# Two units of the joined stage and two of the last feed-forward stage multiplied ahead of their norm

## The chip, the cores and the metric

The kernel runs on one core of one Trainium2 chip. The metric is device time in microseconds of one execution; the time of a kernel is the median of its runs.

## The reference

The reference is three blocks of a transformer on 512 tokens of width 1024, in float32: a block with stick-breaking attention, a block with dilated attention, and a block with adaptive modulation whose mixer joins a gated recurrence (HGRN2) and differential attention. What matters here is the third block (`rmsnorm` divides by the root of the mean square and multiplies a gain):

```python
x = _rmsnorm(h, norm_final)                     # end of the first two blocks
mod = jax.nn.silu(c) @ w_ada[l] + b_ada[l]
sh1, sc1, g1, sh2, sc2, g2 = jnp.split(mod[:, None, :], N_MOD, axis=-1)
u = rmsnorm(h, norm1_w[l]) * (1.0 + sc1) + sh1
proj = u @ w_in[l]                              # f, q, i, g, v, d, k of four heads
...
h = h + g1 * mix
u = rmsnorm(h, norm2_w[l]) * (1.0 + sc2) + sh2
ff = (jax.nn.silu(u @ w_ffn_gate[l]) * (u @ w_ffn_up[l])) @ w_ffn_down[l]
h = h + g2 * ff
```

Every product of the form (norm(h) * scale + shift) @ W has the same value as rstd * ((h * scale) @ W) + shift @ W, since rstd is one number per token.

## The kernel before

Activations lie feature-major: `h`, `xh` and `xl` are eight tiles of 128 features by 512 tokens. A "unit" is a 128-column slice of a weight matrix (1024 x 128, eight blocks of 128 x 128). Each operand is split in a rounded high part and a residue: ScalarE writes `whi` (L334, `split_hi`), VectorE or GpSimd writes `wlo` (L345, `split_lo`), and `product` (L348) issues three matmuls for each block: high by high (L360), high weights by low data (L361), low weights by high data (L362). So a unit is 24 matmuls of 512 columns. Units pass through a ring of three or four slots of `raw`, `whi` and `wlo`; SyncE loads `raw` (L278, L291) when the residue of the unit two before is done. The order on each engine is the order in which its program is written out; semaphores join the engines. `ahead` splits a unit two units before its product.

The phases in order are qkv, o_a, gu0, down0, qkvb, o_b, gu1, down1, duo, mix, gu2, down2. In `down1` (24 units of the second block's feed-forward, three for each tile of `h`) ScalarE and VectorE also form the modulation vector `mod` (`ada_scale`, `ada_product`, `ada_tile`), ScalarE squares each new tile twice (L896, L897) and GpSimd adds the squares up. PE then sums them over the partitions (L758, L760), and from both sums VectorE and ScalarE form `twin`, the root of the two norms in a row (`twin_dve`, `twin_root_act`). `modulate_dve` (L929) multiplies `h` by scale and twin tile by tile, `modulate_act` (L943) adds the shift and writes `xh`, and `lower_dve` (L937) writes `xl`. PE's first unit of duo, f, waits for each tile.

`duo` is the joined stage: four heads with units f, q, i, g, v, d, k. VectorE forms the gates of the recurrence (`gate_first` L1657, `gate_rest`, `scan`), the differences for the decays (`difference`, L1688), and ScalarE the decays (L1297, L1298) and the copies of the products out of PSUM (`unit_out`, L1245). PE turns the copies of i and v (L2064). Behind head 0's sweep the matmuls of the levels (L2009) follow. GpSimd forms a query product (L1101).

`mix` has eight units, one for each tile of `h`; the first four have most of their matmuls done early. `res_dve` (L679) multiplies the old tile by the joined norm (L693), waits for the product and writes the new tile (L700); `res_act` (L658) squares it (L427); GpSimd adds (L457). PE sums (L480), and VectorE (L497, L504, L506, L509) and ScalarE (L485, L487) form `rstd`. The modulation of eight tiles follows as above, and the first unit of `gu2` waits for each tile (`ffn_pe`). `gu2` has eleven rounds of four units (gate, up, gate, up) of which `ffn_dve` and `ffn_act` form the activations.

Of the kernel before, what the change touches and what calls it, by code (L numbers as in the profile page):

```python
# [77 lines left out]
class Units:  # L78
# [3 lines left out]
    def __init__(self, weights, count, body, ring, before, used, widths=None):  # L82
        self.weights, self.count, self.body, self.ring = weights, count, body, ring
        self.first, self.used = before, list(used)
        self.widths = widths or [KT] * body
        self.last = False

# [10 lines left out]
    def slot(self, j):  # L98
        return j % self.body % self.ring
# [7 lines left out]
def build(nc, a, out):  # L107
    ctx = ExitStack()
    with ctx:
# [31 lines left out]
        small = place("small", [P, 96], F32)  # L141
        nc_wada = top[0]
# [7 lines left out]
        plain = [place(f"plain{m}", [P, S], F32, base + 16 * KIB + 2 * KIB * m)[:, :] for m in range(KT)]  # L150
        gained = [place(f"gained{m}", [P, S], F32, base + 32 * KIB + 2 * KIB * m)[:, :] for m in range(KT)]
# [12 lines left out]
        work = small[:, 66:96]  # L164

# [52 lines left out]
        twin = place("twin", [P, S], F32, where["yh"])  # L218
# [16 lines left out]
        oraw = put("oraw", [P, S], F32)  # L235
        amat = place("amat", [P, NB, P], F32, nc_wada)
# [15 lines left out]
        for name, count, body, ring in (("qkv", 8, 3, 3), ("o_a", 2, 4, 4), ("gu0", 11, 4, 4), ("down0", 4, 6, 3),  # L252
# [8 lines left out]
            u.order = (1, 2, 0) if name == "qkvb" else None  # L261
        phases[-1].last = True
# [85 lines left out]
        def product(pe, u, t, j, bank, hi, lo, k0=0, start=True, stop=True, ready=None, midway=None, part=None):  # L348
# [65 lines left out]
        r1a, r1f = Residual(), Residual(scaled=False, alone=False)  # L414
        r2a, r2f = Residual(scaled=False), Residual(scaled=False)

        def residual_hi(act, r, m, gain):
# [6 lines left out]
            act.activation(xh[:, m], h[:, m], ACT.Copy, scale=column(gain, m)).then_inc(r.x_hi.sem, 1)  # L424

# [33 lines left out]
        def twin_squares_pool(pool):  # L459
# [8 lines left out]
            for m in range(KT):  # L468
                load_ada(3 * m + 2, 3 * m + 5)
                if 1 <= m < KT - 1:  # L470
# [3 lines left out]
                    for sums in (plain, gained):  # L474
                        pool.tensor_tensor(sums[0], sums[0], sums[m], ALU.add).then_inc(twin_added, 1)
# [116 lines left out]
        y_hi, y_lo = sem("y_hi"), sem("y_lo")  # L592
        twin_squared, twin_added = sem("twin_squared"), sem("twin_added")
# [64 lines left out]
        def res_act(act, u, r, gain, rooted=True, begun=0, ada=None):  # L658
            per = 1 if u.body == 4 else 3

            def body(t, end=False):
                for j in range(u.body):
                    if not leading(t) or j >= begun:
                        split_hi(act, u, ahead(u, t, j, end))
                    if ada is not None:
                        ada_scale(act, ada, t, j)
                    if j % per == per - 1:
                        m = t * (u.body // per) + (j // per)
                        residual_hi(act, r, m, gain)
                        residual_sq(act, r, m, (j // per) % 2)  # L670
            body(0)
# [7 lines left out]
        def res_dve(dve, u, r, gain, modulation=None, ada=None, regain=None, refined=True, begun=0, banks=EARLY):  # L679
            per = 1 if u.body == 4 else 3  # L680

            def body(t, end=False):
                for j in range(u.body):
                    if not leading(t) or j >= begun:
                        split_lo(dve, u, ahead(u, t, j, end))
                    final = end and j == u.body - 1
# [16 lines left out]
                    if ada is not None and final:  # L703
                        ada_product(dve, ada, t, j)
            body(0)
# [14 lines left out]
        def res_pe(pe, u, r, hi, lo, ready, ada=None, sum_now=True, twin=False, early=0, banks=EARLY):  # L720
# [35 lines left out]
            if twin:  # L756
                pe.wait_ge(twin_squared, 2 * KT - 1)
                pe.matmul(ps[:, 7], ones[:, :], plain[KT - 1], start=False, stop=True).then_inc(twin_total.sem, 1)  # L758
                pe.wait_ge(twin_squared, 2 * KT)
                pe.matmul(ps[:, 6], ones[:, :], gained[KT - 1], start=False, stop=True).then_inc(twin_total.sem, 1)  # L760
# [3 lines left out]
        def ffn_act(act, u, f):  # L764
            def body(t):
                for j in range(4):
                    split_hi(act, u, ahead(u, t, j, False))
                    if j % 2:
# [3 lines left out]
                        act.activation(tmp[i][:, :], tmp[i][:, :], ACT.Silu).then_inc(f.silu.sem, 1)  # L772
                        hold(act, f.prod, n)
                        act.activation(acth[:, 2 * t + i], tmp[2 + i][:, :], ACT.Copy).then_inc(f.hi.sem, 1)  # L774
            with act.Fori(0, u.count) as t:
                body(t)

        def ffn_dve(dve, u, f, scaled=True):
            def body(t):
                for j in range(4):  # L780
                    split_lo(dve, u, ahead(u, t, j, False))
                    if j % 2:
# [4 lines left out]
                        if scaled:  # L787
# [8 lines left out]
                        dve.tensor_tensor(tmp[2 + i][:, :], tmp[i][:, :], tmp[2 + i][:, :], ALU.mult).then_inc(f.prod.sem, 1)  # L796
# [19 lines left out]


# [69 lines left out]
        def twin_squares_act(act, u, r):  # L887

            def body(t, end=False):
                for j in range(u.body):  # L890
                    split_hi(act, u, ahead(u, t, j, end))
                    ada_scale(act, 1, t, j)
                    if j % 3 == 2:
                        m = t * 2 + j // 3
                        wait(act, r.h_new, m + 1)
                        act.activation(plain[m], h[:, m], ACT.Square).then_inc(twin_squared, 1)  # L896
                        act.activation(gained[m], h[:, m], ACT.Square, scale=column("final1", m)).then_inc(twin_squared, 1)  # L897
# [10 lines left out]
        def twin_dve(dve, r):  # L908
# [5 lines left out]
            dve.scalar_tensor_tensor(twin[:, :], ps[:, 6], 1.0 / D, var[:, :], ALU.mult, ALU.add).then_inc(twin_var.sem, 1)  # L914
            wait(dve, twin_root, 2)
# [7 lines left out]
        def modulate_dve(dve, key, scale, shift, factor):  # L923

            for m in range(KT):
# [5 lines left out]
                if m:  # L931
                    lower_dve(dve, key, shift, m - 1)
            lower_dve(dve, key, shift, KT - 1)

        def lower_dve(dve, key, shift, m):
# [4 lines left out]
        def modulate_act(act, key, shift):  # L940
# [1343 lines left out]
```

## Time and profile before

| | us |
|---|---|
| median of 3 runs | 1973.14 (1970.89 to 1973.36) |
| profiled execution | 1972.97 |
| its span, first to last instruction | 1970.8 |
| PE busy | 1904.0 (97%) |
| VectorE busy | 1082.2 (55%) |
| ScalarE busy | 928.4 (47%) |
| GpSimd busy | 138.5 (7%) |

The mean granted clock of PE is 0.989 of 2.4 GHz. "PE busy" counts matmuls that overlap by their pipelined ends, so a share of 97% does not say that PE has only 3% to lose. Times in the rows are microseconds from the start of the span; a row of the timeline has start, duration, engine, line, operation, output and inputs, count, and in brackets the idle time of the engine before it with what ended that time. In the chain of waits a row has start, duration and what.

### The profile page before, as it was taken

To read this page: it belongs to the slowest core of one execution; us is meant where nothing else is said; L and a number is where in the kernel's file an instruction comes from. 1 tells how busy PE (TensorE), PEld (TensorE's weight loads), DVE (VectorE), ACT (ScalarE), POOL (GpSimd) and SP (SyncE) were. 2 spreads that over 40 slices of the span, in tenths; PEclk is the share of its full clock that TensorE was granted. 3 is DMA by queue.
4 is the path that set the end of the run, shared out by engine and by line. 5 is a ranking of instruction groups with operands and counts; after the bars stand their busy time and mean duration, and the time that the engine had idled before them with its cause. 6 is when DMAs were issued, how large, how long until landed. Compare 5 with 4: busy or idle time off the path is not lost.

```text
span 1970.8 us, 25056 instructions
## 1 busy us (share of the span) xinstructions
PE 1904.0 (97%) x8914; PEld 1533.2 (78%) x8914; DVE 1082.2 (55%) x1640; ACT 928.4 (47%) x1520; POOL 138.5 (7%) x132
## 2 busy tenths in 40 slices
PE   7999999999999899999999999889999879999997
PEld 6777778888788677778888878668887658888886
DVE  5566554444466767755444455577776554444322
ACT  5555543323477444444434367556555344343322
POOL 0000020000021000010000013211011100000000
PEclk9999999999999999999999999999999989999999
DMA  3111123232455322223232355511122122323331
GB/s 136 65 64 64 43 93 103 93 103 89 134 195 192 105 86 90 87 76 99 86 105 85 104 170 189 183 64 58 66 70 65 65 74 86 105 85 104 89 98 62
DMA packets 56478, 193.65 MB, mean 98 GB/s; under 512 B 7136, under 2 KB 7648, under 8 KB 56416
## 3 DMA queue, kind: packets, MB, share of 16 engines
q1 hardware_dynamic: 47712, 163.60, 25.5%
q0 software_dynamic: 7696, 27.79, 4.3%
q10 hardware_dynamic: 1008, 1.45, 0.2%
q8 instruction: 37, 0.61, 0.1%
q14 instruction: 25, 0.20, 0.0%
HBM read 186.52 MB, written 2.10 MB: 96 GB/s over the span
## 4 chain that ended last, share of the span: by engine, by line
PE 92%; DVE 3%; ACT 2%; issue 1%; DMA 1%; SPq 0%; ACTq 0%; POOL 0%; DVEq 0%
PE ps L360 27%; PE ps L361 26%; PE ps L362 26%; PE ps L2009 1%; PE ps L1896 1%; PE ps L956 1%; PE ps L1877 1%; PE ps L981 1%; PE ps L1912 1%; PE ps L971 1%; PE ps L1900 1%; DVE xl L937 1%; PE ps L2057 0%; PE ps L2044 0%; PE ps L2083 0%
## 5 line engine op out<-in xcount | busy, mean ns | idle before, releaser
L360 PE MATMUL ps<-xh,whi 128*128 128x512 f32 x1536 | 608.5, 396 | 22.9 <-DVE xl L937 16.6
L362 PE MATMUL ps<-xh,wlo 128*128 128x512 f32 x1536 | 600.7, 391 | 0.0
L361 PE MATMUL ps<-xl,whi 128*128 128x512 f32 x1536 | 600.3, 391 | 0.0
L345 DVE TENSOR_TENSOR wlo<-raw,whi 128x1024 fp32r<-128x1024 f32 (+1 forms) x296 | 365.5, 1244 | 231.3 <-ACT whi L334 225.7
L334 ACT ACTIVATE whi<-raw 128x1024 fp32r<-128x1024 f32 (+1 forms) x304 | 312.0, 1036 | 170.0 <-PE ps L362 169.1
L360 PEld LDWEIGHTS ps<-xh,whi 128*128 128x128 f32 x1536 | 289.8, 189 | 93.1 <-issue 16.8
L362 PEld LDWEIGHTS ps<-xh,wlo 128*128 128x128 f32 x1536 | 289.9, 189 | 61.3
L361 PEld LDWEIGHTS ps<-xl,whi 128*128 128x128 f32 x1536 | 290.1, 189 | 59.6 <-issue 1.4
L360 PE MATMUL ps<-acth,whi 128*128 128x512 f32 x528 | 213.0, 403 | 0.0
L362 PE MATMUL ps<-acth,wlo 128*128 128x512 f32 x528 | 208.6, 395 | 0.0
L361 PE MATMUL ps<-actl,whi 128*128 128x512 f32 x528 | 208.3, 394 | 0.0
L772 ACT ACTIVATE tmps<-tmps 128x512 f32<-128x512 f32 x66 | 41.7, 632 | 306.8 <-DVE tmps L788 207.3
L457 POOL TENSOR_TENSOR sqsum<-sqsum,tmps 128x512 f32<-128x512 f32 x39 | 52.0, 1333 | 951.2 <-ACT tmps L427 951.2
L362 PEld LDWEIGHTS ps<-acth,wlo 128*128 128x128 f32 x528 | 99.3, 188 | 23.3
L361 PEld LDWEIGHTS ps<-actl,whi 128*128 128x128 f32 x528 | 99.6, 189 | 21.4 <-issue 0.2
L360 PEld LDWEIGHTS ps<-acth,whi 128*128 128x128 f32 x528 | 99.6, 189 | 21.3 <-issue 0.2
L788 DVE TENSOR_TENSOR tmps<-ps,rstd 128x512 f32<-128x512 f32 x44 | 30.4, 692 | 133.3 <-PE ps L362 133.3
L360 PE MATMUL ps<-oh,whi 128*128 128x512 f32 x192 | 78.6, 409 | 6.5 <-DVE wlo L345 3.5
L798 DVE TENSOR_TENSOR actl<-tmps,acth 128x512 f32 (+1 forms) x66 | 45.7, 693 | 65.2 <-ACT acth L774 65.2
L361 PE MATMUL ps<-ol,whi 128*128 128x512 f32 x192 | 77.1, 402 | 0.0
L362 PE MATMUL ps<-oh,wlo 128*128 128x512 f32 x192 | 76.7, 400 | 0.0
L774 ACT ACTIVATE acth<-tmps 128x512 f32 x66 | 41.7, 632 | 66.3 <-DVE tmps L796 66.3
(296 smaller groups left out, 2230.8 us busy)
## 6 DMA issues: line engine op xcount, KB each, us to landing
raw<-in_gu SPq DMA_DIRECT2D x132, 512.0 KB, 3.3
raw<-in_down SPq DMA_DIRECT2D x48, 512.0 KB, 3.7
raw<-in_qkv SPq DMA_DIRECT2D x24, 512.0 KB, 4.3
wada<-in_ada POOLq DMA_DIRECT2D x24, 512.0 KB, 3.7
tmps<-in_ada POOLq DMA_DIRECT2D x24, 512.0 KB, 3.6
raw<-in_qkvb SPq DMA_DIRECT2D x24, 512.0 KB, 3.6
raw<-in_down SPq DMA_DIRECT2D x24, 384.0 KB, 3.1
raw<-in_recur SPq DMA_DIRECT2D x16, 512.0 KB, 3.3
```

Source lines behind the costliest of these rows:

```text
L334: act.activation(whi[:, s, 0:n], raw[:, s, 0:n], ACT.Copy).then_inc(hi_done, 1)
L345: eng.tensor_tensor(wlo[:, s, 0:n], raw[:, s, 0:n], whi[:, s, 0:n].bitcast(F32), ALU.subtract).then_inc(lo_done, 1)
L360: pe.matmul(ps[:, bank], whi[:, s, w], hi[:, k0 + k], start=start and k == 0, stop=False)
L361: pe.matmul(ps[:, bank], whi[:, s, w], lo[:, k0 + k], start=False, stop=False)
L362: mm = pe.matmul(ps[:, bank], wlo[:, s, w], hi[:, k0 + k], start=False, stop=stop and k == n - 1)
L457: pool.tensor_tensor(sqsum[:, :], sqsum[:, :], sq[m % 2][:, :], ALU.add).then_inc(r.added.sem, 1)
L772: act.activation(tmp[i][:, :], tmp[i][:, :], ACT.Silu).then_inc(f.silu.sem, 1)
L774: act.activation(acth[:, 2 * t + i], tmp[2 + i][:, :], ACT.Copy).then_inc(f.hi.sem, 1)
L788: dve.tensor_tensor(tmp[i][:, :], ps[:, 2 * i], rstd[:, :], ALU.mult).then_inc(f.gate.sem, 1)
L798: dve.tensor_tensor(actl[:, 2 * t + i], tmp[2 + i][:, :], acth[:, 2 * t + i].bitcast(F32), ALU.subtract).then_inc(f.lo.sem, 1)
L937: dve.scalar_tensor_tensor(xl[:, m], tmp[m % 2][:, :], mod[:, shift + m:shift + m + 1], xh[:, m].bitcast(F32), ALU.add, ALU.subtract).then ...
L956: pe.matmul(tri_ps[i][:, OFF[b]:OFF[b] + w], q[rows, c * P:(c + 1) * P], k[rows, 0:w], start=True, stop=True, skip_group_check=True)\
```

## The change

Two units of `duo` (f and q of head 0) and two units of `gu2` (the first gate and up) are multiplied with `xh`, `xl` that hold h * scale without norm and shift. ScalarE writes that `xh` (`raw_hi`) and VectorE that `xl` (`raw_lo`) as each tile of `h` is new, in `down1` and in `mix`. The norm is applied to the products: VectorE multiplies f, q, gate and up by `twin` or `rstd`, and a bias per feature, shift @ W, comes in with ScalarE's function or VectorE's product. The biases are matmuls of two columns (high part and residue of the shift) with the weights of both units (`shift_products`, 32 of them), issued inside the first unit ahead of its last block. The sums over the partitions move into the middle of the first unit. The modulated tiles are still made, for all later units; `modulate_act` waits until the second raw unit has read a tile. The units of the ring are split further ahead (two or three more splits at the end of `down1` and `mix`, with slots 2 and 3 of duo exchanged). The squares of `down1` now share two buffers, `root(r1f)`, the second half of `mod` and the refinement of the joined norm come later in VectorE's and ScalarE's programs, and GpSimd's loads of tables wait for the sums.

The core of the diff:

```diff
@@ product
+                if k == n - 1 and late is not None:
+                    late()
...
+                if read is not None and k < n - 1:
+                    mm.then_inc(read, 1)
@@ new functions
+        def raw_hi(act, r, m, scale):
+            act.activation(xh[:, m], h[:, m], ACT.Copy, scale=scale[:, bass.ds(m, 1)]).then_inc(r.x_hi.sem, 1)
+        def raw_lo(dve, r, m, scale):
+            wait(dve, r.x_hi, m + 1)
+            dve.scalar_tensor_tensor(xl[:, m], h[:, m], scale[:, bass.ds(m, 1)], xh[:, m].bitcast(F32),
+                                     ALU.mult, ALU.subtract).then_inc(r.x_lo.sem, 1)
+        def shift_products(pe, u, n, bank):
+            pe.wait_ge(shift_lo, n + 1)
+            for j in range(2):
+                pe.wait_ge(lo_done, u.number(0, j) + 1)
+                for k in range(KT):
+                    w = slice(k * P, (k + 1) * P)
+                    for part in (whi, wlo):
+                        mm = pe.matmul(ps[:, bank, 2 * j:2 * j + 2], part[:, u.slot(j), w], shifts[n][:, k, :],
+                                       start=k == 0 and part is whi, stop=k == KT - 1 and part is wlo, skip_group_check=True)
+                mm.then_inc(biased, 1)
+        def biases(dve, n, bank, sign):
+            dve.wait_ge(biased, 2 * n + 2)
+            dve.tensor_copy(bias_parts, ps[:, bank, 0:4]).then_inc(bias_step, 1)
...
@@ twin_squares_act (down1, ScalarE)
                     split_hi(act, u, ahead(u, t, j, end))
+                    if end and j == u.body - 1:
+                        split_hi(act, U["duo"], (0, 2), freed=8)
...
+                        act.activation(plain[not first], h[:, m], ACT.Square).then_inc(twin_squared, 1)
+                        act.activation(gained[not first], h[:, m], ACT.Square, scale=column("final1", m)).then_inc(twin_squared, 1)
+                        raw_hi(act, r, m, raw)
@@ twin_dve
+            split_lo(dve, U["duo"], (0, 3))
             wait(dve, twin_root, 2)
@@ modulate_act
+                if m == 3 and between is not None:
+                    between()
                 act.wait_ge(n_scaled[key], m + 1)
+                if m < KT - 1:
+                    act.wait_ge(raw_read, read_before[key] + m + 1)
+                else:
+                    act.wait_ge(mm_done, u.number(0, 1) + 1)
@@ GpSimd, tables
-            pool.wait_ge(mm_done, u.first)
+            wait(pool, twin_total, 2)
@@ ScalarE, duo
+            def gate_out():
+                act.wait_ge(raw_scaled, 1)
+                act.wait_ge(bias_step, 3)
+                act.activation(cum, kd[:, :], ACT.Exp, scale=-1.0, bias=bias[:, 0:1]).then_inc(duo_out, 1)
+            def query_out():
+                act.wait_ge(raw_scaled, 2)
+                act.activation(hq[:, :], qd[:, :], ACT.Identity, bias=bias[:, 1:2]).then_inc(duo_out, 1)
+            modulate_act(act, "1", 0, (tmp[3], tmp[4]), u, gate_out)
...
                     gate_inverse(n)
+                    if n == 0:
+                        act.wait_ge(n_lo["1"], KT)
+                        root(act, r1f)
+                        wait(act, r1f.root, 2)
+                        shift_high(act, 1)
@@ VectorE, duo
+            raw_out("f", 2, kd)
+            biases(dve, 0, 5, -1.0)
+            modulate_dve(dve, "1", scale1, 0, twin, (tmp[3], tmp[4]))
...
                     gate_first(n)
+                if n == 0:
+                    stage_norm()
...
                     difference(n, (0, 1))
+                if n == 0:
+                    raw_out("q", 3, qd)
+                    refine_rest(dve, r1f)
+                    shift_low(dve, 1)
@@ mix and gu2, ScalarE
-            res_act(act, U["mix"], r2a, None, begun=2)
-            modulate_act(act, "2", 24)
-            ffn_act(act, U["gu2"], f2)
+            res_act(act, U["mix"], r2a, None, begun=2, rooted=False, raw=scale2,
+                    extra=lambda: split_hi(act, U["gu2"], (0, 2), freed=3))
+            split_hi(act, U["gu2"], (0, 3), freed=3)
+            root(act, r2a)
+            modulate_act(act, "2", 24, (tmp[0], tmp[1]), U["gu2"])
+            ffn_act(act, U["gu2"], f2, raw=True)
@@ mix and gu2, VectorE
+            res_dve(dve, U["mix"], r2a, None, modulation=16, regain="final1", begun=2, banks=EARLY_MIX, refined=False,
+                    raw=scale2, extra=lambda: split_lo(dve, U["gu2"], (0, 2)))
+            refine_var(dve, r2a, 7)
+            split_lo(dve, U["gu2"], (0, 3))
+            refine_rest(dve, r2a)
             wait(dve, r2a.rstd, 4)
+            biases(dve, 1, 5, 1.0)
+            modulate_dve(dve, "2", scale2, 24, rstd, (tmp[0], tmp[1]))
+            dve.wait_ge(n_lo["2"], KT)
+            ffn_dve(dve, U["gu2"], f2, scaled=False, raw=True)
@@ TensorE, duo
+                if j == 0:
+                    product(pe, u, 0, j, 2, xh, xl, ready=r1f.x_lo, midway=lambda: twin_totals(pe),
+                            late=lambda: shift_products(pe, u, 0, 5))
+                    for part_of in (4, 5):
+                        ada_tile(pe, 1, 3, part_of)
+                    return
+                if j == 1:
+                    product(pe, u, 0, j, 3, xh, xl, read=raw_read)
+                    return
@@ TensorE, gu2
+            wait(pe, r.h_new, 5)
+            product(pe, u, 0, 0, 0, xh, xl, ready=r.x_lo, midway=lambda: total(pe, r, 7),
+                    late=lambda: shift_products(pe, u, 1, 5))
+            wait(pe, r.h_new, 6)
+            product(pe, u, 0, 1, 1, xh, xl, read=raw_read)
```

## Rows read from the trace of the kernel before

**Rows 1.** The page's part 4, chain that ended last: share of each engine.
```profile
PE 92%; DVE 3%; ACT 2%; issue 1%; DMA 1%; SPq 0%; ACTq 0%; POOL 0%; DVEq 0%
```

**Rows 2.** Waits of PE, 1262 to 1326: total, times, longest, in us.
```profile
PE ps L360 <- DVE xl L937: 8.2, 4, 6.7
...
PE ps L360 <- DVE wlo L345: 2.5, 1, 2.5
```

**Rows 3.** Waits of PE, 1545 to 1625.
```profile
PE ps L360 <- DVE xl L937: 8.4, 5, 6.7
...
PE ps L360 <- DVE wlo L345: 3.5, 1, 3.5
```

**Rows 4.** Timeline of the first norm: start, duration, engine, line; two rows of the chain.
```profile
1272.61 0.69 DVE L698 TENSOR_TENSOR h<-ps,h 128x512 f32<-128x512 f32 x1 [3.75 <-PE ps L362]
...
1273.87 0.71 ACT L897 ACTIVATE gained<-h,vec 128x512 f32<-128x512 f32 x1
...
1274.02 1.12 PE ps L758 x2
...
1275.14 0.87 PE ps L760 x2
...
1280.64 1.42 DVE L929 SCALAR_TENSOR_TENSOR tmps<-h,small,twin 128x512 f32<-128x512 f32 x2
...
1292.57 0.50 PE L360 MATMUL ps<-xh,whi 128*128 128x512 f32 x1
```

**Rows 5.** Timeline behind it, gate chain to the turn of i.
```profile
1297.59 0.42 DVE L1657 TENSOR_SCALAR tmps<-tmps 128x512 f32<-128x512 f32 x1
...
1305.53 1.23 DVE L345 TENSOR_TENSOR wlo<-raw,whi 128x1024 fp32r<-128x1024 f32 x1 [0.32 <-ACT whi L334]
...
1306.67 2.38 DVE L1688 TENSOR_TENSOR levels<-tmps 128x512 f32<-128x512 f32 x2
...
1306.06 1.83 POOL L1101 TENSOR_TENSOR wada<-hq,tmps 128x512 f32<-128x512 f32 x1 [27.32 <-ACT hq L1245]
...
1309.11 0.58 ACT L1245 ACTIVATE tmps<-ps 128x512 f32<-128x512 f32 x1
...
1314.04 0.60 PE L2064 MATMUL ps<-ident,tmps 128*128 128x128 f32 x4
```

**Rows 6.** Small operations: timeline, and a row of the chain for L1896.
```profile
1953.21 0.95 PE L2168 MATMUL ps<-ones,sqsum 128*128 128x1 f32 x8
...
1961.78 0.17 DVE L1826 TENSOR_TENSOR small<-small 128x4 f32<-128x4 f32 x1 [0.51 <-ACT small L1415]
...
238.54 0.24 PE ps L1896 x2
```

**Rows 7.** Timeline in the mix stage.
```profile
1549.55 1.04 ACT L334 ACTIVATE whi<-raw 128x1024 fp32r<-128x1024 f32 x1
...
1550.62 1.45 DVE L345 TENSOR_TENSOR wlo<-raw,whi 128x1024 fp32r<-128x1024 f32 x1 [1.64 <-ACT whi L334]
...
1552.21 0.47 PE L360 MATMUL ps<-oh,whi 128*128 128x512 f32 x1 [3.46 <-DVE wlo L345]
...
1554.15 1.04 ACT L334 ACTIVATE whi<-raw 128x1024 fp32r<-128x1024 f32 x1
```

**Rows 8.** Timeline of the second norm.
```profile
1576.49 0.75 DVE L700 SCALAR_TENSOR_TENSOR h<-ps,mod,h 128x512 f32<-128x512 f32 x1 [0.60 <-PE ps L362]
...
1579.35 1.17 PE L480 MATMUL ps<-sqsum,ones 128*128 128x512 f32 x2 [2.97 <-POOL sqsum L457]
...
1584.79 1.42 DVE L929 SCALAR_TENSOR_TENSOR tmps<-h,small,rstd 128x512 f32<-128x512 f32 x2
...
1596.72 0.49 PE L360 MATMUL ps<-xh,whi 128*128 128x512 f32 x1
```

**Rows 9.** Stretches: length, busy time by engine, PEclk the granted clock.
```profile
1597.52:1608.46 10.94, 10.94 (x50) 1.00 0.30 98
...
1307.00:1313.00 6.00, 6.00 (x20) 4.81 (x21) 5.93 (x10) 5.11 (x9) 0.90 (x1) 0.72 0.54 172
```

More of the change, by code:

```diff
@@ L86, in __init__ @@
         self.last = False
+        self.places = tuple(range(ring))
     def per(self, slot):
@@ L98, in slot @@
     def slot(self, j):
-        return j % self.body % self.ring
+        return self.places[j % self.body % self.ring]
     def landings(self, t, j):
@@ L235, in build @@
         oraw = put("oraw", [P, S], F32)
+        twin = place("twin", [P, S], F32, where["hgate1"])
         amat = place("amat", [P, NB, P], F32, nc_wada)
@@ L346, in split_lo, with product @@
                               ALU.subtract).then_inc(lo_done, 1)
-        def product(pe, u, t, j, bank, hi, lo, k0=0, start=True, stop=True, ready=None, midway=None, part=None):
+        def product(pe, u, t, j, bank, hi, lo, k0=0, start=True, stop=True, ready=None, midway=None, part=None,
+                    late=None, read=None):
             pe.wait_ge(lo_done, u.number(t, j) + 1)
@@ L664, in body @@
                         split_hi(act, u, ahead(u, t, j, end))
+                    if extra is not None and end and j == u.body - 1:
+                        extra()
                     if ada is not None:
@@ L685, in body @@
                         split_lo(dve, u, ahead(u, t, j, end))
+                    if extra is not None and end and j == u.body - 1:
+                        extra()
                     final = end and j == u.body - 1
@@ L704, in body @@
                         ada_product(dve, ada, t, j)
+                    if raw is not None and j % per == per - 1:
+                        raw_lo(dve, r, m, raw)
             body(0)
@@ L813, in ffn_pe, with raw_ffn_pe, body @@
             body(0)
+            with pe.Fori(1, u.count) as t:
+                body(t)
+        def raw_ffn_pe(pe, u, f, r, key):
+            def body(t):
+                for j in range(4):
+                    wait(pe, f.up, 2 * t + (j // 2 - 1))
+                    product(pe, u, t, j, j, xh, xl, ready=n_lo[key] if leading(t) and j == 2 else None)
+            wait(pe, r.h_new, 5)
[3 more added lines that the diff above has]
+            product(pe, u, 0, 1, 1, xh, xl, read=raw_read)
+            for j in (2, 3):
+                product(pe, u, 0, j, j, xh, xl, ready=n_lo[key] if j == 2 else None)
             with pe.Fori(1, u.count) as t:
@@ L1313, in _ @@
                     head_root(2 * t - 1)
-                if more:
+                if t >= 0 and more:
                     high("f", n)
@@ L1765, in _ @@
                     picks(t, range(4, 8))
-                if more:
+                if t >= 0 and more:
                     low("f", n)
@@ L1990, in dense @@
                 last_in[bank] = j
-                product(pe, u, 0, j, bank, xh, xl, ready=n_lo["1"] if j == 0 else None)
+                product(pe, u, 0, j, bank, xh, xl, ready=n_lo["1"] if j == 2 else None)
             def level_scores(t):
```

154 lines of the change are left out of this document (98 added, 56 removed).

## The prediction

> **What bounds the kernel.** I read the chain of waits first: the matrix engine (PE) holds 92% of it [rows 1]. So only PE's idle time and its slow stretches can be won. PE's waits by stretch come second. Around the norm ahead of the joined stage it waits 8.2 us for modulated tiles and 2.5 us for weights [rows 2]; around the norm ahead of the last feed-forward stage 8.4 and 3.5 us [rows 3], and 2.97 us for the last sum of squares [rows 8]. Third, the order of time there: each norm is a serial chain over VectorE (DVE) and ScalarE (ACT), and then eight tiles are modulated at 1.45 us each while the first unit follows tile by tile. A dense unit alone takes 5.47 us, 0.228 a matmul (48 in 10.94 us) [rows 9].
>
> The change fills the two waits with two units each. Their end is then set by other things, which is what has to be worked out. I call the places A (joined stage) and B (last feed-forward).
>
> **Place A, PE.** The last product of down1 ends at 1272.57, DVE adds it at 1272.61 [rows 4]. f's tiles 0 to 6 are ready, so PE goes on: 12 matmuls to 1275.2, the two sums (1.99 us for the pair; their inputs are ready at 1274.6) [rows 4] to 1277.1, 9 matmuls to 1279.1, then the 32 matmuls of two columns, new here. Their price: eight one-column matmuls lie in 0.95 us, 0.11 each with their weight loads, and 128-column ones of this weight type run at 0.12 [rows 6]. Lower bound 0.10; upper 0.228, as if each cost a dense one. I take 0.112, since the loads are the same: 3.6 us, to 1282.7. Tile 7 follows (ACT scales it behind the two squares, by 1275.3, DVE by 1276.2: no wait) and f ends at 1283.5.
>
> By the Trainium skill ("TensorE: Matmul & The Clock Gate", section "Back-to-back issue gap") a matmul of 1 to 64 columns needs only some 25 ns, which would be 0.8 us for the 32. Rows 6 speak against it where each has its own weight load; it is rival 4.
>
> **Place A, the modulation.** The norm's own chain ran from the sums' end (1276.0) to 1280.64 [rows 4]; it moves by 1.2 to 1281.9, and the residue of unit 3 lies in its wait for ACT. So f's end decides: DVE multiplies f (0.69 [rows 4]) and forms the biases, three small operations of about 0.2 with their gaps (0.17 alone [rows 6]; bounds 0.5 and 2.1, as if full width): modulation starts at 1284.9, 4.3 later than before. ACT's wait for q's reads costs nothing: q runs from 1284.0 at 0.69 a tile, modulation at 1.45. q ends at 1289.4, i then follows the tiles: f's tile 7 began 11.93 after the modulation [rows 4], so i's begins at 1296.8 and i ends at 1297.5. Before, i ended at 1304.1. That is 6.6 us ahead, and g's weights are already split, so the 2.5 us wait [rows 2] goes too: g ends at 1303.0.
>
> **What is late next.** The turn of i waits for ACT's copy of it, behind the first two decays and decay 2, behind DVE. The gate chain starts 0.9 earlier (1296.7 against 1297.59 [rows 5]), as the root, the mod columns and the refinement now stand behind it. From it to the third difference lay 9.08 us, of which 1.14 and a wait of 0.32 were q's residue [rows 5]: both go, so 1304.3. In comes q's multiplication 0.69, three refinement steps of 0.73, the small shift 0.2: 1307.4. GpSimd's query product lies there now; before it lay on two differences, and they took 2.38 [rows 5] where two operations of that width and engine take 1.4 [rows 4], so 1.0 more (bounds 0 and 1.83): 1308.4. Then one difference 0.7, a decay of two halves 0.7 (both as wide as one such operation), copy 0.58 [rows 5]: the turn at 1310.4 against 1314.04 [rows 5], 3.6 earlier. But PE has waited 7.4 us. After the 2.5 us wait before, the mean clock of 1307 to 1313 was 0.72 [rows 9], a stretch at 1.2 instead of 2.4 GHz that costs (1 - 0.72) x 6 = 1.7 to 1.8 us. The old one falls on g, ahead of 1314.04; the new falls on v, behind. **A gives 3.6 - 1.8 = 1.8 us.** The sweep of levels has slack, as v now ends under two us earlier than it did.
>
> Beside PE, at no price: down1 gets one ACT scaling and one DVE residue per tile, against 15 us of PE work a tile; the tables' four GpSimd transfers start 4.4 us later, and the scan that wants them is 20 us off; SP's queue gets units 4 and 5 free earlier. Were this cover gone, a late table would cost its lateness one for one.
>
> **Place B, the mix stage.** Here the cover is thin. DVE and ACT alternate in a ring of 4.60 us per unit [rows 7] beside PE's 5.5. Before the first split stand two tiles: for tile 0 the ring gets ACT's scaling and DVE's residue (a scaled pass of ACT takes 0.71 [rows 4], the residue as long as h's update, 0.75 [rows 8], and DVE no longer works while ACT squares: 2.1), for tile 1 a scaling (0.63, as passes on one engine overlap by some 0.1). The split of unit 4 goes from 1549.55 to 1552.3 and, with its residue free of GpSimd's addition (1.45 [rows 7] becomes 1.23), PE restarts at 1554.7, not 1552.21 [rows 7]: **2.5 us lost**. Unit 7 ends at 1578.9. The ring itself becomes 4.60 + 0.63 - 0.22 = 5.0. Its sixth split stands at 1552.3 + 25.0 = 1577.3; behind it two residues instead of one, the regain, and h(7) is written from 1581.4, not 1576.49 [rows 8]: 4.9 late, and the ring is now the bound.
>
> **Place B, the rest.** PE does half of gate 0 to 1581.7, waits 2.6 us, sums from 1584.3 (1579.35 + 4.9 [rows 8]) to 1585.3, 9 matmuls to 1587.4, in the slow clock again 1.8 more, 1589.2; 32 two-column ones to 1592.8; biases 0.6: modulation at 1593.4 against 1584.79 [rows 8], 8.6 late. (The norm is ready at 1589.7.) Gate 1 follows 11.93 later with its last tile [rows 8], so unit 3 begins at 1596.72 + 8.6 + 0.8 = 1606.1. Before it began two units after 1597.52, at 1608.46 [rows 9]. 2.3, less 0.1 for the first product of the loop, whose Silu, product and splits all stand behind the modulation: **B gives 2.2 us.**
>
> **Sum:** 1.8 + 2.2 = 4.0. The profiled execution took 1972.97 (span 1970.8); 1969.0 is left. The median of the runs is 0.17 higher, 1973.14, so 1969.1.
>
> **Rivals.** (1) PE's clock holds through B's short wait, or GpSimd costs DVE nothing in A. For: the sums of B ran at near full rate after 2.97 us of idle [rows 8]. Against: rows 9. Worth 1.8 and 1.0: 1967.3 or 1968.1, both 1966.3.
>
> (2) The two-column matmuls leave the array so idle that the clock falls in them. Tile 7 then costs 0.7 more and up to half of the 3.6 us doubles, 0.7 to 2.5 at each place, on the path in both: 1972 in the middle. For: nothing here shows 3.6 us of such matmuls. Against: eight of them [rows 6] cost nothing. The Trainium skill ("TensorE: Matmul & The Clock Gate", section "The HAM clock gate") has the clock go by how busy the array has been, throttled unless activity releases it; by that rule this rival would hold, and no row here decides it.
>
> (3) Slower: each two-column matmul costs its weight load and then a fill, 0.228. Both groups grow from 3.6 to 7.3, and both stand ahead of a modulation: 4.0 - 7.4 = -3.4, 1976.5. Break-even is 0.112 + 4.0/64 = 0.175. Rows 6 speak against it.
>
> (4) They cost 25 ns. Then the norm's chain decides: 1.7 won in A (1281.9 + 1.3 = 1283.2), 2.8 in B: 1964.6. No row supports it.
>
> (5) A gives nothing, since DVE's order behind the gate chain is later by two more us than I add up, or the early units don't start early because a split of theirs waits; B alone stays: 1970.9.
>
> **Numbers.** Forecast 0.50 (own range 1967.5 to 1971), rivals 0.19, 0.15, 0.08, 0.02, 0.06. 0.2% is 3.9 us, so the border is 1969.2 and the forecast lies on it. Faster: half of 0.50, all of (1) and (4), 0.46, and 0.01 of (5); within: the other half, (2), most of (5), 0.43; slower: (3) and a tail of (2), 0.10. Range 1965.0 to 1974.0: it leaves out (3), (4) and tails.
>
> **What would show it.** 32 matmuls of two columns in about 3.6 us with the granted clock at 1.0; modulation in A from 1284.9; a wait of PE for ACT's copy of i of 7 us, ended at 1310.4; in B a restart of unit 4 at 2.5 us later than before, h(7) 4.9 later, a wait of 2.6 us ahead of the sum, modulation 8.6 later. Times in B are against A's end, which itself moves by 1.8. I am wrong if PE's wait in A ends on something else, if h(7) in B is still bound by PE, or if the spacing of the two-column matmuls is far from 0.11.

## The result, and the profile after

The changed kernel takes 1962.81 us (median of 5 runs, 1961.45 to 1963.79), the kernel before 1973.36 beside it (1970.89 to 1973.87): a ratio of 0.9945, 95% interval 0.9934 to 0.9957. I had said 1969.1 (1965.0 to 1974.0). It is faster, as forecast, but by 10.6 us and not by 4, and outside my range. The profiled execution took 1961.45, its span is 1959.6.

The first look is at where the 11.2 us between the two spans lie. Each mark below is the start of an instruction that both kernels have, read from the timeline.

| stage, us | before | after |
|---|---|---|
| start to the update of h(7) by down1 | 1272.61 | 1263.52 |
| A: to the first matmul on the levels | 53.22 | 52.61 |
| joined stage, to the first update of h by mix | 219.52 | 219.48 |
| B: mix and gu2, to the first matmul of down2 | 286.12 | 287.27 |
| down2, to its last update of h | 127.02 | 124.20 |
| tail | 12.31 | 12.52 |

9.1 us came ahead of place A, 2.8 in down2, behind place B. The two places that were rebuilt gave 0.6 and took 1.2. Of the 9.1 us, 6.6 were there at the first matmul of down1 (1141.55 before, 1134.99 after), ahead of all code of the change; in down1 itself ScalarE and VectorE have one operation more for each tile, PE has the same matmuls. So the question is about code that nobody changed. Grouped by line and shape (busy time, mean ns of one), the groups of the kernel before that differ are

```profile
L360 PE MATMUL ps<-xh,whi 128*128 128x512 f32 x1536 | 608.5, 396 | 22.9 <-DVE xl L937 16.6 <-DVE wlo L345 3.2 <-ACT h L1134 2.2
...
L360 PE MATMUL ps<-acth,whi 128*128 128x512 f32 x528 | 213.0, 403 | 0.0
L362 PE MATMUL ps<-acth,wlo 128*128 128x512 f32 x528 | 208.6, 395 | 0.0
L361 PE MATMUL ps<-actl,whi 128*128 128x512 f32 x528 | 208.3, 394 | 0.0
```

and in the changed kernel

```profile
L369 PE MATMUL ps<-xh,whi 128*128 128x512 f32 x1536 | 610.3, 397 | 5.1 <-ACT h L1248 3.2 <-DVE rstd L1591 0.8 <-DVE wlo L351 0.8
...
L369 PE MATMUL ps<-acth,whi 128*128 128x512 f32 x528 | 210.6, 399 | 0.0
L370 PE MATMUL ps<-actl,whi 128*128 128x512 f32 x528 | 206.0, 390 | 0.0
L371 PE MATMUL ps<-acth,wlo 128*128 128x512 f32 x528 | 205.6, 389 | 0.0
```

Matmuls on xh are as they were; every one on acth or actl is 4 to 6 ns shorter, and so are those on oh, ol, yh and yl (2544 in all). The change has one line that reaches them: `top[0] += 128`, which reserves the two shift tiles ahead of `wada`. Every tile allocated behind it, acth, oh and yh too, stands 128 bytes higher. The duration of a matmul in a profile is partly modelled, so here is the distance from one start to the next as well, in the dense stretches of the two traces: on acth 0.2328 us before and 0.2273 after, on xh 0.2273 and 0.2270.

The waits of PE (total, times, longest) show what the change did at its two places. Place A, 1262 to 1326, where [rows 2] had 8.2 and 2.5:

```profile
PE ps L2234 <- ACT tmps L1372: 6.7, 1, 6.7
PE ps L369 <- DVE xl L1045: 0.2, 1, 0.2
```

Place B, 1535 to 1625, where [rows 3] had 8.4 and 3.5:

```profile
PE ps L369 <- DVE wlo L351: 6.7, 1, 6.7
PE ps L534 <- POOL sqsum L511: 4.0, 1, 4.0
```

Both waits for modulated tiles are gone, and others stand in their place. The granted clock (the column after the counts in brackets: length, then PE, PEld, DVE, ACT, POOL busy, PEclk, DMA share, GB/s) shows the rest of the bill:

```profile
1270.00:1273.00 3.00, 3.00 (x30) 3.00 (x29) 2.07 (x3) 0.00 (x0) 0.79 (x2) 1.00 0.96 310
1273.00:1280.00 7.00, 7.00 (x22) 5.83 (x22) 4.22 (x9) 1.48 (x3) 1.06 (x2) 0.51 0.30 119
...
1302.00:1308.00 6.00, 6.00 (x19) 4.82 (x18) 5.93 (x15) 5.94 (x10) 0.00 (x0) 0.56 0.28 87
1581.00:1584.00 3.00, 3.00 (x28) 3.00 (x28) 0.85 (x2) 0.00 (x0) 0.00 (x0) 0.95 0.39 153
1584.00:1588.00 4.00, 4.00 (x12) 3.34 (x13) 1.82 (x5) 0.11 (x1) 0.00 (x0) 0.50 0.00 0
```

In these stretches PE is busy throughout, and at 1.2 GHz behind the two-column matmuls (from 1273 and 1584) and behind the wait for i's copy (from 1302).

### The profile page after: what moved, and what is told of

Read it like the earlier page. It is cut to its first block, busy times and chain, and to the rows that moved or that the text cites. A ratio compares the mean times of both kernels' runs of the same rounds, so it can differ in the third digit from the quotient of the medians.

```text
span 1959.6 us, 25235 instructions
## 1 busy us (share of the span) xinstructions
PE 1899.3 (97%) x8978; PEld 1543.4 (79%) x8978; DVE 1105.4 (56%) x1666; ACT 909.8 (46%) x1517; POOL 137.7 (7%) x132
## 4 chain that ended last, share of the span: by engine, by line
PE 90%; DVE 4%; ACT 2%; issue 1%; DMA 1%; SPq 0%; ACTq 0%; POOL 0%; DVEq 0%
PE ps L369 26%; PE ps L370 26%; PE ps L371 26%; PE ps L2179 1%; PE ps L2059 1%; PE ps L1070 1%; PE ps L2040 1%; PE ps L2075 1%; PE ps L1095 1%; PE ps L1085 1%; DVE wlo L351 1%; PE ps L2063 1%; DVE xl L1045 1%; PE ps L2227 0%; PE ps L2214 0%
## 5 line engine op out<-in xcount | busy, mean ns | idle before, releaser
L511 POOL TENSOR_TENSOR sqsum<-sqsum,tmps 128x512 f32<-128x512 f32 x39 | 51.9, 1331 | 945.1 <-ACT tmps L481 945.1
L849 ACT ACTIVATE acth<-tmps 128x512 f32 (+1 forms) x66 | 41.7, 632 | 66.0 <-DVE tmps L879 65.1
```

Source lines behind the costliest of these rows:

```text
L511: pool.tensor_tensor(sqsum[:, :], sqsum[:, :], sq[m % 2][:, :], ALU.add).then_inc(r.added.sem, 1)
```

## The experiments

Two theories of the gain. **Placement:** the 128 bytes, and nothing else, make the matmuls on acth, oh and yh faster. **Reordering:** the gain is the change's own. Ratios are against the kernel before on the same chip, with 95% intervals. Stages below are those of the table above; each comes from one profiled execution of its kernel.

**gap_ahead** and **gap_again**, the kernel before and one line:

```diff
+        top[0] += 128
         nc_wada = top[0]
```

> The kernel before with nothing of the change but 128 unused bytes of SBUF ahead of wada, so that wada, tmps, acth, actl, oh, ol, yh, yl stand 128 bytes higher, as in the changed kernel. Theory (placement): the first 1272 us of the changed kernel run 9.1 us faster in code that is the same, because matmuls that read acth or oh as moving operand are 5 ns shorter; so here the span falls by about 12 us (9.1 up to the end of down1, 2.8 in gu2 and down2), to some 1961 us, acth matmuls at 399/390/389 ns instead of 403/395/394. Rival (the time came from the change itself): no change, 1970 to 1974 us.

> The kernel before with 128 unused bytes ahead of wada, again, on the same chip as the changed kernel: the yardstick for the reordering without its placement. 1958 to 1961 us.

1959.93 and 1959.16 us, 0.9934 (0.992 to 0.9948) and 0.9929 (0.9916 to 0.9943). One unused stretch of 128 bytes gives 13 to 14 us, more than the whole change and more than the 12 I expected. 1.3 and 1.6 of it lie in place A, where no matmul reads a moved tile (below, and in the part on the prediction).

**after_unmoved**, the changed kernel with the shift tiles at the end of SBUF (`...` stands for what is left out of a line or between lines):

```diff
-        nc_shifts = top[0]
-        top[0] += 128
...
-        shifts = [place(f"shifts{n}", ..., nc_shifts + 64 * n) for n in range(2)]
         region = top[0]
+        shifts = [place(f"shifts{n}", ..., 228608 + 64 * n) for n in range(2)]
```

> The changed kernel with its two shift tiles at the end of SBUF instead of ahead of wada, so that every other tile stands where it stood before the change. Theory (placement): the gain goes; the reordering itself is worth nothing or a small loss (0.6 us less at the first place, 1.2 more at the second), so 1972 to 1975 us. Rival (the change itself): stays at 1962 to 1963 us.

1971.93, 0.9995 (0.9986 to 1.0004). The reordering with its placement taken away can't be told from no change. Placement stands, the other theory falls.

**gap_region** has the 128 bytes behind `tmps`, **gap256** has 256 ahead of `wada`.

> The kernel before with 128 unused bytes behind tmps instead of ahead of wada: acth, actl, oh, ol, yh, yl move by 128 bytes, wada and tmps don't. If the moving operands' own place decides, about 1961 us as with the gap ahead of wada. If the place of wada or tmps (which ScalarE, VectorE and GpSimd read and write beside the matmuls) decides, 1970 to 1974 us.

> The kernel before with 256 unused bytes ahead of wada: the tiles start at 0 modulo 512 bytes (256 in the kernel before, 384 with 128 bytes). If only the old place is bad, about 1961 us; if only the new place is good, 1972 us or more; in between if the cost follows the distance to the weights' tiles (128 modulo 512) or to a boundary.

gap_region: 1958.69, 0.9924 (0.9909 to 0.9939). It is acth, oh and yh, not wada or tmps. gap256: 1972.89, 0.9998 (0.9988 to 1.0007). A start at 0 modulo 512 is as slow as one at 256. That leaves two rules, the moving tile's own start, or its distance to the tile that holds the weights.

**all_moved** (`base` + 128) and **weights_moved** (`top[0] += 128` ahead of `whi`) set them against each other.

> The kernel before with the start of all its SBUF tiles moved up by 128 bytes: acth, oh, yh then start at 384 modulo 512 (as in the changed kernel), but h, xh, xl, whi and wlo at 256 instead of 128. Matmuls that read acth ran 0.232 us apart with acth at 256 or 0, and 0.227 us apart with it at 384; those that read xh (at 128) 0.227 us. Theory 1 (a moving operand that starts on a multiple of 256 bytes costs 5 ns a matmul): the acth, oh and yh ones get their 0.227, and the 4608 dense matmuls that read xh or xl go to 0.232, about 25 us in all: 1980 to 1988 us. Theory 2 (the distance to the weights' tile counts, good where it is a multiple of 256): nothing changes, 1970 to 1975 us.

> The kernel before with 128 unused bytes ahead of whi: h, xh, xl and raw stay at 128 modulo 512, whi and wlo go from 128 to 256, acth, oh and yh from 256 to 384. Theory 1 (the moving operand's start alone): 1958 to 1961 us. Theory 2 (the distance to the weights' tile): all dense matmuls become slow, 1992 to 2000 us.

1971.76, 0.9998 (0.9988 to 1.0007), and 1996.05, 1.0122 (1.0105 to 1.0139). The distance decides, the moving tile's own start does not. In weights_moved, xh has not moved at all, whi and wlo have, and now its matmuls are slow too (0.2325 us from start to start):

```profile
L361 PE MATMUL ps<-xh,whi 128*128 128x512 f32 x1536 | 616.3, 401 | 21.9 <-DVE xl L938 15.9
...
L362 PE MATMUL ps<-xl,whi 128*128 128x512 f32 x1536 | 608.1, 396 | 0.0
L361 PE MATMUL ps<-acth,whi 128*128 128x512 f32 x528 | 213.0, 403 | 0.0
L362 PE MATMUL ps<-actl,whi 128*128 128x512 f32 x528 | 208.2, 394 | 0.0
```

The same groups in all_moved, where xh moved along with the weights, and acth stands at 384, the "good" place of the changed kernel, but 128 from them:

```profile
L361 PE MATMUL ps<-xl,whi 128*128 128x512 f32 x1536 | 600.4, 391 | 0.0
...
L360 PE MATMUL ps<-acth,whi 128*128 128x512 f32 x528 | 213.0, 403 | 0.0
L361 PE MATMUL ps<-actl,whi 128*128 128x512 f32 x528 | 208.2, 394 | 0.0
```

**half_way**, 64 bytes, so a distance of 192 modulo 256.

> The kernel before with 64 unused bytes ahead of wada: acth, oh and yh stand 192 modulo 256 bytes from whi and wlo (128 in the kernel before, 0 in the changed one). Moving the weights' tiles alone showed that the distance between the two tiles decides, not the moving tile's own place. If every distance that is no multiple of 256 costs the same, 1970 to 1974 us with acth matmuls at 403/395/394 ns; if the cost is half at half the way, about 1966 us; if only 128 is bad, 1959 us.

1974.56, 1.0005 (0.9995 to 1.0014), acth at 404/395/395. Of the distances tried, 0 modulo 256 is fast, 128 and 192 are not, and 192 is no faster than 128. Other distances were not run.

Now the reordering, whose 4 us are missing. The yardstick is gap_again.

**changed_again**, **first_only** (A alone) and **second_only** (B alone), all with the 128 bytes:

> The changed kernel beside the yardstick. If the reordering is worth what its two places show in the traces (0.6 us won at the first, 1.2 lost at the second), 0 to 2 us above the yardstick; the medians so far say 2.9 above. Rival: the reordering gains its forecast 4 us and another chip hid it, 1955 to 1957 us.

> Only the first place (norm ahead of the joined stage) in the new order, the second as before; shift tiles ahead of wada, so with the 128 bytes. Theory: the 32 two-column matmuls and the slow clock behind them eat most of the gain: 0 to 1 us below the yardstick. Rival (forecast): 1.8 us below it. Rival (the loss sits here): 1 to 2 us above it.

> Only the second place (norm ahead of the last feed-forward stage) in the new order, the first as before, with the 128 bytes. Theory: 1 to 2 us above the yardstick, since h(7) comes 6.7 us later, the matmul on the sum waits 4.0 us for GpSimd and the clock falls again behind the two-column matmuls. Rival (forecast): 2.2 us below it.

1959.68, 1959.23 and 1962.30 us against the yardstick's 1959.16; ratios 0.9936 (0.9923 to 0.995), 0.9931 (0.9917 to 0.9944) and 0.9945 (0.9931 to 0.9958). The intervals of all three overlap the yardstick's. second_only stands 3.1 us above it by the median, more than the 1 to 2 of its theory, and its executions are far apart (1958.18 to 1963.60); the profiled one is the fastest of them. By stage:

| us | A | joined | B |
|---|---|---|---|
| gap_ahead, gap_again | 51.90, 51.64 | 217.88, 219.47 | 286.08, 285.39 |
| changed, changed_again | 52.61, 50.98 | 219.48, 217.88 | 287.27, 287.13 |
| first_only | 52.57 | 219.48 | 285.40 |
| second_only | 51.75 | 217.87 | 285.40 |
| few_products | 48.80 | 219.43 | 283.18 |
| products_early, early_again | 51.02, 52.64 | 217.87, 219.44 | 282.28, 283.21 |
| second_early | 51.75 | 219.46 | 282.36 |
| spread_products | 50.64 | 217.91 | 282.23 |
| split_ahead | 51.40 | 219.47 | 281.32 |
| both_mended | 50.29 | 217.93 | 281.34 |

Rebuilt, A varies from 51.0 to 52.6 about the yardstick's 51.8, B stands 1 to 2 us above it, or level. In the profile of second_only the clock did not fall behind the two-column matmuls, where the changed kernel had 0.50:

```profile
1580.00:1584.00 4.00, 4.00 (x31) 3.80 (x31) 1.93 (x7) 0.00 (x0) 0.00 (x0) 1.00 0.33 115
1584.00:1588.00 4.00, 4.00 (x20) 3.30 (x19) 3.56 (x7) 2.13 (x3) 0.00 (x0) 1.00 0.00 0
```

The B of this profile is 1.9 us shorter than the changed kernel's.

**few_products** (with the start and stop flags of the matmuls to match):

```diff
-                for k in range(KT):
+                for k in range(1):
```

> The changed kernel with 4 two-column matmuls at each place in the place of 32 (leaves out seven eighths of the product of shift and weights, so the biases aren't whole). Theory (these matmuls and the slow clock behind them are where the forecast gain went): 3.2 us at the first place and 3.6 at the second go, and 2 to 3 us at each from the clock; less what the modulation then makes PE wait: 5 to 9 us less than the changed kernel. Rival (the modulation binds already): at most 2 us less.

1953.59, 0.9907 (0.989 to 0.9923), 6 us under changed_again (on another chip). 2 to 4 us in A, where the clock then stays at 1.00, and 4 in B. The stages are what shows it: the 3.2 and 3.6 us of PE work that go are not all won, since PE then waits 2.2 us at A and 1.5 at B for modulated tiles.

**products_early**:

```diff
-            product(pe, u, 0, 0, 0, xh, xl, ready=r.x_lo, midway=lambda: total(pe, r, 7),
-                    late=lambda: shift_products(pe, u, 1, 5))
+            def sum_of_squares():
+                shift_products(pe, u, 1, 5)
+                total(pe, r, 7)
+            product(pe, u, 0, 0, 0, xh, xl, ready=r.x_lo, midway=sum_of_squares)
```

> The changed kernel with the 32 two-column matmuls of its second place issued ahead of the matmul on the sum of squares, where PE stands idle for 4.0 us, instead of ahead of the last slice. Theory: their 3.6 to 4.0 us go from PE's path, and the stretch behind them isn't slowed again: 3 to 5 us less than the changed kernel (1956 to 1958 us). Rival: the modulation and GpSimd's sum set when unit 2 can run, so PE only waits later: within 1 us of the changed kernel.

1954.00, 0.991 (0.9893 to 0.9926), lower than I expected. The same work, in the hole that PE had anyway. Its waits, 1530 to 1602:

```profile
PE ps L369 <- DVE wlo L351: 6.7, 1, 6.7
PE ps L369 <- DVE xl L1050: 1.3, 3, 0.5
PE ps L534 <- POOL sqsum L511: 0.4, 1, 0.4
```

The 4.0 us wait for GpSimd is 0.4, and B falls by 3.9 to 5.0. That is 2.2 to 3.8 us under the yardstick's B: the new order of B was worth its forecast 2.2 and more, with the 32 matmuls in another place. The half of my theory that the stretch behind them isn't slowed did not come true:

```profile
1575.00:1579.00 4.00, 4.00 (x12) 3.15 (x11) 3.50 (x5) 1.26 (x2) 0.53 (x1) 0.57 0.20 63
1579.00:1583.00 4.00, 4.00 (x20) 3.27 (x19) 3.77 (x9) 1.41 (x3) 0.00 (x0) 1.00 0.17 68
```

The changed kernel has a stretch like the first behind its wait for GpSimd (0.61 in 1576 to 1580) and then the longer one from 1584; here only one is left.

**second_early** (the same without A), **spread_products** (products_early, and A's 32 matmuls four at a time; the first diff below) and **split_ahead** (products_early, and mix's unit 4 split first; the second diff, where `raw_turn` says which tiles a turn scales):

```diff
-                    product(pe, u, 0, j, 2, ..., late=lambda: shift_products(pe, u, 0, 5))
+                    product(pe, u, 0, j, 2, ..., each=lambda k: slice_products(pe, u, 0, 5, k))
```

```diff
+            return ((), (), (0,), (1,), (2,), (3, 4), (5, 6), (7,))[m]
...
-                            raw_hi(act, r, m, raw)
+                            for n in raw_turn(u, m):
+                                raw_hi(act, r, n, raw)
...
-                        raw_lo(dve, r, m, raw)
+                        for n in raw_turn(u, m):
+                            raw_lo(dve, r, n, raw)
```

> Only the second place in the new order, with its two-column matmuls ahead of the matmul on the sum of squares; the first place as before, with the 128 bytes. If the first place's new order is worth nothing (first_only stood 0.1 us from the yardstick), as the same with both places: 1953 to 1956 us. Rival (the first place gives its forecast 1.8 us once nothing disturbs it): 1955.5 to 1957.5 us.

> products_early with the first place's 32 two-column matmuls spread over the eight slices of unit 0 (four behind each three dense matmuls) instead of in one run ahead of its last slice. Theory (a run of 3.6 us of them lets the granted clock fall, and the stretch behind it is slow for some 6 us in some executions): the slow stretch at 1273 to 1280 us of the profile goes, 1 to 3 us less than products_early, 1951 to 1953 us. Rival (it falls as well with four at a time, or the modulation binds): within 1 us of products_early.

> products_early with the scaled copies of h(0) and h(1) and their remainders put behind the split of the last stage's unit 4 on ScalarE and VectorE (each later turn takes one up, two turns take two). Theory: PE's 6.7 us wait for the split of unit 4 goes back to the 3.5 us of the kernel before, and PE comes to the sum of squares 2.5 to 3.2 us earlier: 1950.5 to 1952.5 us. Rival (the later copies then hold the ring, or the sum of squares comes no earlier): within 1 us of products_early.

second_early: 1958.83, 0.9929 (0.9912 to 0.9945), its B as in products_early, above the range of my theory and of the rival. The two ran on different chips and their intervals overlap, so what A with its products in one run is worth stays open.

spread_products: 1953.96, 0.9899 (0.9883 to 0.9916). The slow stretch of A is gone, as two windows show,

```profile
1272.00:1276.00 4.00, 4.00 (x28) 3.56 (x26) 3.62 (x5) 1.26 (x2) 2.13 (x4) 1.00 0.60 174
1276.00:1280.00 4.00, 4.00 (x21) 3.36 (x20) 3.38 (x8) 1.39 (x2) 1.50 (x2) 1.00 0.82 282
```

but the median is that of products_early, which ran on another chip, and the intervals overlap. That the spreading keeps the clock up isn't shown by this: split_ahead has the 32 in one run as before, and in its profile the clock holds too,

```profile
1270.00:1274.00 4.00, 4.00 (x31) 3.69 (x29) 3.58 (x5) 1.26 (x2) 2.07 (x4) 1.00 0.60 220
1274.00:1278.00 4.00, 4.00 (x26) 3.56 (x26) 1.86 (x6) 0.07 (x1) 1.50 (x2) 1.00 0.68 238
```

while it fell in the six other profiles with one run of 32 at A, and in neither of the two with the 32 spread. Beside second_early, on one chip, spread_products is 4.9 us lower, and no execution of the one reaches the other's (at most 1955.01, at least 1956.83), though the intervals of the ratios still touch. So the new A, so arranged, very likely gains; its stage shows 1.1 us of it.

split_ahead: 1955.95, 0.991 (0.9894 to 0.9927). The split's wait goes back as expected, while the wait for GpSimd grows,

```profile
PE ps L369 <- DVE wlo L351: 3.5, 1, 3.5
PE ps L534 <- POOL sqsum L511: 2.2, 1, 2.2
```

so B gains 1.0 of the 3.2 us. By the ratio it is the rival.

**both_mended** (all three) beside **early_again**, on one chip:

> The changed kernel with all three amendments: the second place's two-column matmuls ahead of the sum of squares, the first place's spread over the slices of unit 0, and the split of unit 4 ahead of the scaled copies. From the stages of the traces (0.4 us from spreading, 1.0 us from the split, beside products_early): 1952 to 1954 us, 1 to 2 us less than products_early beside it. Rival (both only shift a wait): within 0.5 us of it.

> products_early again on the same chip as both_mended, as its yardstick: 1953 to 1956 us.

1951.38, 0.9892 (0.9877 to 0.9907), against 1956.78, 0.9921 (0.9908 to 0.9935). More than I expected: 5.4 us by the medians, 3.9 between the two profiled executions. The stages of these show 2.35 in A, 1.9 in B, 1.5 in the joined stage, and 2.4 the other way ahead of A; the last two have the same code in both kernels (see the end), and of the 2.35 in A only 0.7 are left against products_early's own 51.02. It is the best version, 21 us under the kernel before on its chip, some 13 of them from the 128 bytes, which gave as much alone.

## Why the prediction was wrong

**The step that failed** is the one that had no term. "Beside PE, at no price" and the sum took every dense matmul outside the two places at the rate of the kernel before. Neither speaks of the line that reserves 128 bytes and moves acth, oh and yh. It was worth 13.2 us (1973.11 to 1959.93, gap_ahead), three times the sum, and with its placement taken away the changed kernel isn't faster (1971.93 against 1973.11, 0.9986 to 1.0004). That it came out faster, as forecast, is luck. No rival held it either: all five were about the two places.

**The price of a two-column matmul** was right: 0.112 forecast; 32 took 3.67 us in A and 4.02 in B, 0.111 apart while the clock was full:

```profile
1273.00 0.25 PE L466 MATMUL ps<-shifts,wlo 128*128 128x2 f32 x1
1273.12 0.35 PE L466 MATMUL ps<-shifts,whi 128*128 128x2 f32 x1
1273.33 0.35 PE L466 MATMUL ps<-shifts,wlo 128*128 128x2 f32 x1
1273.54 0.78 PE L369 MATMUL ps<-xh,whi 128*128 128x512 f32 x1
```

Rivals 3 and 4 fall. The same rows are **rival 2**, to which I gave 0.15: the spacing goes from 0.11 to 0.21 within the run, and the dense matmuls behind it follow at half the clock. I charged the doubling of the two-column matmuls themselves; what is slowed is mostly the dense work behind them, 7 us at 0.51, (1 - 0.51) x 7 = 3.4 us of clock. Not all of it stands on the path. In A the turn of i comes 38.2 us after h(7) with this fall, 37.9 with one half as long (changed_again) and 37.0 with none (split_ahead): 1.2 us. In B it is the 1.9 us between the changed kernel and second_only. So the rival's price, 0.7 to 2.5 at each place, held, by another way than I gave. The Trainium skill ("TensorE: Matmul & The Clock Gate", section "The HAM clock gate") says that the clock follows how busy the array has been. This trace agrees, with 1.00 until 1273 and 0.51 behind, and few_products, with four such matmuls, kept 1.00; split_ahead kept 1.00 with all 32, so the fall isn't certain. I had set that rule against eight matmuls of [rows 6], too few to speak.

**A, the order of time,** was right. From down1's update of h(7) the modulation starts 12.8 us on (12.3 forecast), the turn of i 38.2 (37.8), after a wait of 6.7 (7.4):

```profile
1263.52 0.69 DVE L763 TENSOR_TENSOR h<-ps,h 128x512 f32<-128x512 f32 x1 [2.04 <-PE ps L371]
...
1276.33 1.41 DVE L1037 SCALAR_TENSOR_TENSOR tmps<-h,small,twin 128x512 f32<-128x512 f32 x2
...
1301.71 1.09 PE L2234 MATMUL ps<-ident,tmps 128*128 128x128 f32 x4 [6.74 <-ACT tmps L1372]
```

What it bought was not quite. The turn came 3.2 us earlier, not 3.6, and the clock behind it cost (1 - 0.56) x 6 = 2.6 us, not 1.8; 0.6 is left of 1.8. In changed_again less of the stretch is slow and 2.2 are left. after_unmoved, where acth stands as in the kernel before, has 51.03, 2.2 less too. So against the kernel before the forecast of A lies between these. But the 128 bytes give 1.3 to 1.6 of it alone, and the two don't add up: in gap_ahead the same wait of 2.5 us for weights is followed by a clock of 1.00, where before had 0.74, and A takes 51.9 instead of 53.2 with the same instructions. Before, then gap_ahead:

```profile
1308.61:1312.61 4.00, 4.00 (x15) 3.21 (x14) 3.93 (x8) 3.92 (x7) 0.00 (x0) 0.74 0.53 170
```

```profile
1301.00:1305.00 4.00, 4.00 (x22) 3.31 (x20) 3.93 (x9) 3.88 (x8) 0.00 (x0) 1.00 0.48 167
```

It is hardly the chance of one execution: the old A takes 53.2 or 53.3 us in all four profiles where acth stands at a slow distance and xh at the fast one (before, gap256, half_way, all_moved), with the clock down behind this wait, and 51.6 to 51.9 in all five with the 128 bytes (gap_ahead, gap_again, gap_region, second_only, second_early), with the clock up. weights_moved, where both stand at a slow distance, has it up too, in 52.0. Why the placement changes the clock there, no run shows. Against the yardstick A's 1.8 comes to nothing: seven rebuilt A with the 32 in one run take 51.0 to 52.6, 51.8 in the mean, the five 51.7. That is rival 5's figure for A, by another cause.

**B, the mix stage:** each term has the right place and is too small.

```profile
1536.91 0.75 DVE L765 SCALAR_TENSOR_TENSOR h<-ps,mod,h 128x512 f32<-128x512 f32 x1 [0.56 <-PE ps L371]
...
1538.97 1.25 DVE L444 SCALAR_TENSOR_TENSOR xl<-h,small,xh 128x512 fp32r<-128x512 f32 x1 [1.31 <-ACT xh L439]
...
1545.51 0.77 PE L369 MATMUL ps<-oh,whi 128*128 128x512 f32 x1 [6.67 <-DVE wlo L351]
...
1573.34 0.75 DVE L765 SCALAR_TENSOR_TENSOR h<-ps,mod,h 128x512 f32<-128x512 f32 x1
...
1576.22 1.44 PE L534 MATMUL ps<-sqsum,ones 128*128 128x512 f32 x2 [4.02 <-POOL sqsum L511]
...
1585.58 1.40 DVE L1037 SCALAR_TENSOR_TENSOR tmps<-h,small,rstd 128x512 f32<-128x512 f32 x2
```

I priced the scaled residue at 0.75, as h's update in [rows 8]; it takes 1.25 to 1.28 in each of the eight turns, where GpSimd's addition of the square overlaps it each time. In down1 the same line takes 1.13 to 1.28 in the six turns with an addition of GpSimd beside it and 0.75 in the two without. So the restart comes 8.6 us after h(0) where [rows 7] make it 5.4 (1546.78 to 1552.21): 3.2 late, not 2.5. The ring is 5.22, not 5.0; h(7) is 36.4 after h(0) instead of 29.7, 6.7 late, not 4.9; the wait ahead of the sum 4.0, not 2.6; the modulation 48.7 after h(0) instead of 38.0, 10.7 late, not 8.6. These 2.1 us of lateness and the 1.9 of clock behind the two-column matmuls (some of it stands in the 2.1 already) cover the way from my 2.2 us won to the 1.2 lost. What I did not ask is why the 32 matmuls stood behind a hole of their own length; products_early does, and gets more than the forecast.

## What to carry to other kernels

A line that reserves memory is a part of the change: list which tiles it moves, and take the rate of a matmul from a row with the same pair of tiles at the same distance. When unchanged code gets faster, compare the groups by line and shape first, and test with a gap of the same size. Here a wait that was filled gave its time back only in part, since the clock fell behind the cheap matmuls and behind the next wait; and 32 cheap matmuls cost B 4 to 5 us less in a hole that PE had anyway than behind it.

## What the runs showed of the hardware

Each dense matmul whose moving tile starts at a distance of 0 modulo 256 bytes from the tile of the weights runs some 5 ns faster than at 128 or 192 (0.2273 against 0.2328 us from start to start on acth; 13.2 us over 2544 of them, 5.2 ns each, though the medians also hold A's 1.3; weights_moved, where the 4608 on xh and xl become slow, 23.9 us, 5.2 ns each). The Trainium skill ("SBUF — State Buffer", section "Operand start alignment") asks only for a start at a multiple of the element size and says of itself that it is about legality and not speed; here the speed differs among starts that all meet it. Why, no run here shows.

The same code has two clocks. In the joined stage PE waits 2.2 us for VectorE's `dprob` near its end; in gap_ahead the clock stays at 1.00 behind it, in gap_again it falls (first gap_ahead, then gap_again):

```profile
1514.80:1522.80 8.00, 5.79 (x31) 4.66 (x30) 7.13 (x13) 3.13 (x4) 0.00 (x0) 1.00 0.43 131
```

```profile
1516.00:1524.00 8.00, 5.79 (x24) 4.51 (x23) 7.06 (x13) 3.13 (x4) 0.00 (x0) 0.79 0.40 131
```

8 x 0.21 = 1.7 us, and the stage takes 217.9 or 219.5 us in every profile of the tables, never between. Both are the same kernel, and I don't know what decides; a single profile can't tell 1.6 us from nothing. The stages above, one profile each, are to be read with that in mind.
